# A hybrid decoder step on one core: the last expert block goes to a fifth plane of rows, four planes are summed by matrix products, and gate products move to the front of compression

## Chip, cores, metric

One Trainium2 chip, one of its cores. The metric is device time in microseconds (us) of one execution. GB/s and MB are decimal.

## What is computed

One layer of a decoder for 512 prompt tokens and 32 sample tokens (544 rows of 1024 values): projections, three gated branches (causal pooling, sparse attention, attention into a memory), an output product, and a mixture of experts. Two pieces of the reference matter here. The first makes the keys and values of the compressed branch from blocks of tokens, for 8 cached sequences and the prompt:

```python
sub = kv[:, :n_sub * CMP_STRIDE].reshape(b, n_sub, CMP_STRIDE, 2, NSA_KV_HEADS, HEAD_DIM)
for r in range(r_sub):
    part = jnp.einsum("bnjcgd,cjde->bncge", sub + pe_r, cmp_w[:, sl])[:, r:r + n_cmp]
```

The second is the end of the experts. Each row goes to 4 of 32 experts, and its four results are added, with gates, to the row itself:

```python
y = jnp.zeros((a, d), h.dtype).at[order].set(out_rows[dest]).reshape(n, TOP_K, d)
return jnp.einsum("nk,nkd->nd", gates, y)
x = x + moe(rmsnorm(x, p["norm2_g"]), p)
```

## The kernel before

The program is a row of phases with a barrier of all engines between them. Each engine has its own list of instructions, written out by hand; engines wait for each other by semaphores, and each engine carries out its list in order, its DMA issues among it. SBUF is one array (`arena`) whose regions are reused by hand; the trace names it `arena` throughout.

**Compression** (L1096 to L1341). For each of 8 sequences s, TensorE forms `products(s, 0)` and `products(s, 1)` (L1298) from cache pages that SP, ScalarE and GpSimd load, `blocks(s)` (L1311) and `keys(s)` (L1319, a transpose of `kn`). ScalarE's `after` (L1167 to L1170) and VectorE's `after` (L1240 to L1247) make `kn`, for which `keys` waits. ScalarE also issues page loads and loads of constants between its instructions (L457, L1200 to L1208). Into this phase five `gate_product`s (L1327) are put as filling: each is 16 products of 272 columns into two banks, which VectorE copies out (L1254) and ScalarE writes to memory (`scr_gate`, L1211). The order on TensorE for s from 1 to 5 is: products(s, 0), blocks(s-1), products(s, 1), keys(s-1), gate_product(s-1). TensorE starts with a wait for `s_bh`, VectorE's first instruction of the phase (L1232), and for weights (`s_cw`). The loads of the next phase (`in_cache_slc` on SP and GpSimd) wait until all five gate results are in memory (`f_s`).

**Gates and output product** (L2351 to L2638). 24 units of gate and branch products on TensorE (L2618, L2625), a sigmoid of ScalarE for each (L2417), VectorE multiplies and adds; SP loads the weights.

**Experts** (L2799 to L3062). Rows are packed into blocks of 96 slots, each block with one expert; with these inputs 32 blocks are used of 54 that the loops allow for. For each used block SP loads 12.6 MB of weights in three pieces into three ring slots (L2817), TensorE forms gate and up products (L2987) and down products (L3013) in three groups g of 32 slots, and ScalarE scales the result (L2906). GpSimd gathers the rows of the next block (L2853) and scatters this block's result (L2874) into `y_of`, which has one plane of rows for each of a row's 4 choices; `slot_row` holds where each slot goes. After the last used block each engine still steps through the unused turns of its loop.

At the end SP waits until all scatters of all blocks have landed (L2823), then loads the four planes of each tile of 128 rows (tile 4 has 32) and stores the finished tiles. VectorE adds the four planes to `x` one after another (L2969), the last tile in two halves of 512 columns (L2977). The list of VectorE:

```python
for n in ORDER[:-1]:
    for k in range(TOPK):
        if k % 2 == 0:
            dve.wait_ge((y_lo, y_hi)[k // 2][n], 16)
        ins = dve.tensor_tensor(x_end(n)[0:r], x_end(n)[0:r], four(n)[0:r, k], ALU.add)
```

Here `ORDER` is tile 4, then 0 to 3, and `four(n)` holds 4 planes of 1024 values on each of 128 partitions.

Of the kernel before, what the change touches and what calls it, by code (L numbers as in the profile page):

```python
# [22 lines left out]
D = 1024  # L23
# [4 lines left out]
NT = 5  # L28
# [189 lines left out]
def build_program(nc, i, o, stop_after=99):  # L218

    ctx = ExitStack()  # L220
    with ctx:
# [881 lines left out]
        with nc.Block() as block:  # L1103
# [50 lines left out]
            def _(act):  # L1154
# [33 lines left out]
                for s in range(NS):  # L1188
# [41 lines left out]
            def _(dve):  # L1230
# [17 lines left out]

                for s in range(NS - 1):
                    after(s)  # L1250
                    if s < FILL:
                        for h in range(2):
                            dve.wait_ge(f_p, 2 * s + h + 1)
                            dve.tensor_copy(fill_out[:, s, HALF * h:HALF * h + HALF], bank(h)[:, 0:HALF]).then_inc(f_e, 1)  # L1254
# [8 lines left out]
            def _(pe):  # L1263
                pe.wait_ge(s_bh, 1)
                pe.wait_ge(s_cw, 48)

# [1008 lines left out]
        b_down = take(D)  # L2275
        assert cursor[0] <= w_gb_at, cursor[0]
        scr_h = scratch("scr_h", [NTOK, D])
        y_of = scratch("y_of", [TOPK, 1024, D])
        hT_at = oT_at - 120 - KD * NTOK
        ring_at = [hT_at, tail_base + KD * D, tail_base]  # L2280
        end_at = [hT_at, hT_at + 4096, w_gb_at, tail_base + KD * D, tail_base + KD * D + 4096]
# [69 lines left out]
        with nc.Block() as block:  # L2351
# [55 lines left out]
            def _(act):  # L2407
                for u in range(24):
# [8 lines left out]
                    act.activation(two(sig[:, s]), gate, ACT.Sigmoid).then_inc(g_sg, 1)  # L2417
                for n in range(NT):
# [15 lines left out]
            def _(dve):  # L2434
                link = linked(dve, s_d5, [0])
                for u in range(24):
# [120 lines left out]
                dve.tensor_copy(n_used[:, 0:1], ends[:, NE - 1:NE])  # L2557

# [186 lines left out]
        cur_gate = take(4)  # L2745
        assert cursor[0] <= routing_base
# [20 lines left out]
        y_hi = [sem(f"y_hi{n}") for n in range(NT)]  # L2767
        y_half = [sem(f"y_half{h}") for h in range(2)]
        y_add = sem("y_add")
# [4 lines left out]
        ORDER = [NT - 1] + list(range(NT - 1))  # L2774
        GU_K = RING_W // 2048
# [3 lines left out]
        four = lambda n: arena[:, end_at[n]:end_at[n] + 4096].rearrange("p (k n) -> p k n", k=TOPK)  # L2779
        x_end = lambda n: x[:, n]  # L2780
        out_p = o["y_prompt"][0]
# [4 lines left out]
        def used(eng):  # L2786

            return eng.value_load(n_used[0:1, 0:1], min_val=1, max_val=NBLK)  # L2788
# [10 lines left out]
        with nc.Block() as block:  # L2799
            @block.sync  # L2800
            def _(sp):
                blocks = used(sp)
                sp.wait_ge(e_sent, 1)
# [18 lines left out]
                for g in range(G):  # L2822
                    sp.wait_ge(e_out[g], blocks * 16)  # L2823
                for n in ORDER[:-1]:
                    r = ROWS[n]
                    sp.dma_start(four(n)[0:r, 0:2], y_of[0:2, 128 * n:128 * n + r].rearrange("k t n -> t k n")  # L2826
                                 ).then_inc(y_lo[n], 16)
                    sp.dma_start(four(n)[0:r, 2:4], y_of[2:4, 128 * n:128 * n + r].rearrange("k t n -> t k n")  # L2828
                                 ).then_inc(y_hi[n], 16)
                last = ORDER[-1]  # L2830
                for h in range(2):
                    sp.dma_start(four(last)[:, :, 512 * h:512 * h + 512],
                                 y_of[:, 128 * last:128 * last + 128, 512 * h:512 * h + 512].rearrange("k t n -> t k n")
                                 ).then_inc(y_half[h], 16)
                for m, n in enumerate(ORDER[:-1]):
                    r = ROWS[n]
                    sp.wait_ge(y_done, m + 1)
                    sp.dma_start(out_p[128 * n:128 * n + 128] if r == 128 else out_s, x_end(n)[0:r]).then_inc(p_out, 16)
                for h in range(2):
                    sp.wait_ge(y_done, NT + h)  # L2840
                    sp.dma_start(out_p[128 * last:128 * last + 128, 512 * h:512 * h + 512], x_end(last)[:, 512 * h:512 * h + 512]
                                 ).then_inc(p_out, 16)
                sp.wait_ge(p_out, 16 * NT + 16)

            @block.gpsimd
            def _(pool):
# [13 lines left out]
                blocks = used(pool)  # L2860
                with pool.Fori(0, NBLK // 9) as nine:  # L2861
                    with pool.If(9 * nine < blocks):
                        with pool.Fori(0, 9) as one:
                            b = 9 * nine + one
                            with pool.If(b < blocks):
# [5 lines left out]
                                for g in range(G):  # L2871
# [3 lines left out]
                                                            y_rows[:, g], None, bounds_check=4 * 1024 * TOPK - 1, oob_is_err=False  # L2875
# [40 lines left out]
            def _(dve):  # L2916
# [13 lines left out]
                blocks = used(dve)  # L2930
                with dve.Fori(0, NBLK // 9) as nine:
# [31 lines left out]
                link = linked(dve, y_add, [0])  # L2963
                for n in ORDER[:-1]:
                    r = ROWS[n]
                    for k in range(TOPK):
                        if k % 2 == 0:
                            dve.wait_ge((y_lo, y_hi)[k // 2][n], 16)
# [107 lines left out]
```

## Time and profile before

| | us |
|---|---|
| median of 3 runs | 1854.88 (1852.64 to 1856.59) |
| the profiled execution, its own time | 1856.81 |
| its span, first to last instruction | 1854.8 |
| compression, first to last product | 175.5 to 300 |
| units of gates | 499 to 706 |
| experts, first to last product of TensorE | 815.6 to 1817.9 |
| behind the last product | 1817.9 to 1854.8 |

The profile is of one execution. Times in rows count from the span's start. PE is TensorE's products, PEld its weight loads, DVE VectorE, ACT ScalarE, POOL GpSimd, SP the engine that only issues DMAs; a q behind a name is the engine's issuing part. A float32 product appears as two rows of the trace.

### The profile page before, as it was taken

What the parts mean: (1) busy time and instruction counts of PE and PEld (TensorE: products, weight loads), DVE (VectorE), ACT (ScalarE), POOL (GpSimd) and SP (SyncE); (2) the same over time, 40 slices, a digit from 0 to 9 for tenths busy, and PEclk for the clock granted to TensorE, in tenths of its full rate; (3) what the DMA queues carried; (4) which work ended last, traced back from release to release, by engine and by line L of the source; (5) the groups of instructions that cost most, each with busy time, mean ns of one, the idle gap of its engine ahead of it and who ended that gap; (6) DMA issues with size and microseconds to landing.
All of it is one profiled execution on the core that took longest, in us unless ns stands there. A gap on an engine that the chain in (4) does not pass through costs nothing.

```text
span 1854.8 us, 40016 instructions
## 1 busy us (share of the span) xinstructions
PE 1714.4 (92%) x16080; PEld 953.3 (51%) x16080; DVE 550.5 (30%) x1391; ACT 338.1 (18%) x740; POOL 449.9 (24%) x520
## 2 busy tenths in 40 slices
PE   7998997679799999879999999999999999999992
PEld 3446785244478884534465754444444444444441
DVE  1333113446401113453232313231323232323235
ACT  3232112146400001101111111111111111111110
POOL 1122326647400006011212212221212222222220
PEclk9997997779999999879999999999999999999996
DMA  9534757850251103339999999999999999999986
GB/s 342 198 104 150 252 162 221 278 210 2 84 165 57 52 25 119 139 151 404 425 422 425 416 421 411 428 423 421 422 421 408 427 423 420 423 420 406 430 338 248
DMA packets 86641, 541.98 MB, mean 292 GB/s; under 512 B 19888, under 2 KB 44048, under 8 KB 73617
## 3 DMA queue, kind: packets, MB, share of 16 engines
q1 hardware_dynamic: 64809, 498.50, 66.8%
q0 software_dynamic: 14544, 32.03, 5.1%
q10 hardware_dynamic: 7232, 10.73, 1.8%
q8 instruction: 32, 0.52, 0.1%
q14 instruction: 24, 0.20, 0.0%
HBM read 523.39 MB, written 29.78 MB: 298 GB/s over the span
## 4 chain that ended last, share of the span: by engine, by line
PE 54%; DMA 1%; DVE 0%; issue 0%; SPq 0%; POOLq 0%; POOL 0%; ACT 0%
PE psum L2987 36%; PE psum L3013 18%; DMA arena<-y_of 1%; PE psum L2997 0%; DVE arena L2977 0%; SPq L2826 0%; SPq L2828 0%; DMA y_of<-arena 0%; DMA arena<-scr_h,arena 0%; DVE arena L2920 0%; POOL arena L2857 0%; POOLq L2788 0%; ACT arena L2906 0%; POOLq L2861 0%; POOLq L2857 0%
## 5 line engine op out<-in xcount | busy, mean ns | idle before, releaser
L2987 PE MATMUL psum<-arena 128*32 128x512 f32 x6144 | 668.2, 592 | 2.7 <-issue 2.7
L2987 PEld LDWEIGHTS psum<-arena 128*32 128x32 f32 x6144 | 234.4, 108 | 417.0 <-issue 413.3
L3013 PE MATMUL psum<-arena 128*32 128x256 f32 x6144 | 344.9, 378 | 0.0
L3013 PEld LDWEIGHTS psum<-arena 128*32 128x32 f32 x6144 | 236.0, 109 | 110.0 <-issue 9.6
L2942 DVE TENSOR_TENSOR arena<-psum,arena 128x512 f32<-128x512 f32 x96 | 66.5, 692 | 582.4 <-PE psum L2987 582.4
L2874 POOL DMA_INDIRECT y_of<-arena x96 | 97.0, 1011 | 476.2 <-ACT arena L2906 476.2
L2902 ACT ACTIVATE arena<-arena 128x256 f32<-128x256 f32 x96 | 40.1, 418 | 610.1 <-DVE arena L2944 610.1
L2618 PE MATMUL psum<-arena 128*128 128x272 f32 x608 | 144.3, 395 | 1.6 <-PEq L235 1.6
L2618 PEld LDWEIGHTS psum<-arena 128*128 128x128 f32 x608 | 116.1, 191 | 28.5 <-issue 3.3
L2853 POOL DMA_INDIRECT arena<-scr_h,arena x96 | 98.8, 1030 | 48.9 <-POOL arena L2849 28.2
L878 PE MATMUL psum<-arena 128*128 128x512 f32 (+1 forms) x256 | 97.4, 541 | 12.7 <-DMA arena<-in_w_tok 10.1
L2906 ACT ACTIVATE arena<-psum,arena 128x256 f32<-128x256 f32 x96 | 45.7, 476 | 245.7 <-PE psum L3013 245.7
L878 PEld LDWEIGHTS psum<-arena 128*128 128x128 f32 x256 | 46.1, 200 | 62.7 <-issue 60.6
L1984 POOL TENSOR_SCALAR arena<-arena 128x512 f32<-128x512 f32 (+3 forms) x64 | 68.5, 1085 | 20.0 <-DVE arena L2111 20.0
L462 POOL DMA_INDIRECT arena<-in_cache_slc,arena x60 | 59.2, 987 | 49.9 <-DMA scr_gate<-arena 26.2
L2444 DVE TENSOR_TENSOR arena<-psum,arena 128x544 f32<-128x544 f32 x24 | 17.4, 725 | 181.3 <-ACT arena L2417 174.6
L2849 POOL COPY arena<-arena 128x3 uint32 x32 | 6.1, 189 | 268.2 <-DMA y_of<-arena 238.1
L2920 DVE STREAM_TRANSPOSE arena<-arena 128x768 f32<-128x768 f32 x33 | 32.2, 977 | 120.5 <-DMA arena<-scr_h,arena 120.5
L2625 PE MATMUL psum<-arena 128*128 128x272 f32 x256 | 63.2, 398 | 3.6 <-DMA arena<-in_w_up 3.6
L462 POOL DMA_INDIRECT arena<-in_cache_cmp,arena x48 | 46.6, 970 | 76.1 <-PE psum L1298 33.8
L440 POOL CAST arena<-arena 32x8 bf16<-32x8 f32 (+1 forms) x6 | 6.2, 1033 | 240.7 <-DMA arena<-in_b_gu 219.8
L1298 PE MATMUL psum<-arena 128*128 128x256 f32 x256 | 61.2, 393 | 3.1 <-DVE arena L1232 3.1
(369 smaller groups left out, 1520.5 us busy)
## 6 DMA issues: line engine op xcount, KB each, us to landing
arena<-in_w_gu SPq DMA_DIRECT2D x64, 4096.0 KB, 15.1
arena<-in_w_down SPq DMA_DIRECT2D x32, 4096.0 KB, 14.5
arena<-in_w_gb SPq DMA_DIRECT2D x24, 512.0 KB, 4.5
arena<-y_of SPq DMA_DIRECT2D x8, 1024.0 KB, 15.3
arena<-in_cache_cmp SPq DMA_DIRECT2D x62, 128.0 KB, 3.1
arena<-in_cache_slc SPq DMA_DIRECT2D x60, 128.0 KB, 6.5
arena<-in_x_all SPq DMA_DIRECT2D x8, 512.0 KB, 11.3
arena<-in_w_tok SPq DMA_DIRECT2D x2, 2048.0 KB, 14.0
```

The lines of the kernel that those rows point to most:

```text
L462: pool.indirect_dma_start(dst, None, i[table], bass.IndirectOffsetOnAxis(page_row[:, at:at + 1], 0)).then_inc(sem, 16)
L878: mm = pe.matmul(bank(2 + c)[0:r, 0:b - a], dstT(n)[:, k], w_tok[:, k, a:b], start=(k == 0), stop=(k == KD - 1))
L1298: mm = pe.matmul(sum_bank(s, c)[:, 0:2 * n].rearrange("p (g b m) -> p g b m", g=2, b=PAGES), w_cmp[:, c, j], turned, start=(j == 0), stop= ...
L1984: ins = pool.tensor_scalar(rows, rows, c[:, g:g + 1], None, ALU.mult)
L2618: pe.matmul(bank(4 * s + h)[:, 0:HALF], w_gb[:, u % 6, k], hT[:, k, t], start=(k == 0), stop=(k == KD - 1))
L2625: mm = pe.matmul(bank(4 * s + 2 + h)[:, 0:HALF], w_up[:, k, 128 * c:128 * c + 128], oT_of(k)[:, t], start=(k == k0), stop=(k == k1 - 1))
L2853: pool.indirect_dma_start(xg[:, g], None, h_quarters, bass.IndirectOffsetOnAxis(row_from[:, g:g + 1], 0), bounds_check=4 * NTOK - 1, oob_i ...
L2874: pool.indirect_dma_start(y_quarters, bass.IndirectOffsetOnAxis(row_to[:, g:g + 1], 0), y_rows[:, g], None, bounds_check=4 * 1024 * TOPK - ...
L2906: act.activation(y_rows[:, g], dn_half(g), ACT.Copy, scale=cur_gate[:, g:g + 1]).then_inc(e_yc, 1)
L2942: dve.tensor_tensor(gu_c[:, g], gu_bank(g), bias_sb, ALU.add).then_inc(e_ba, 1)
L2987: mm = pe.matmul(gu_bank(g)[32 * j:32 * j + 32].rearrange("p (h n) -> p h n", h=2), xgT[:, g, 32 * k:32 * k + 32], gu_w(slot)[:, part, :, ...
L3013: mm = pe.matmul(dn_half(g)[32 * j:32 * j + 32], actT[:, g, 32 * k:32 * k + 32], dn_w(slot)[:, part, 256 * j:256 * j + 256], start=(k == 0 ...
```

## The change

Compression: `gate_product(0)` stands first on TensorE, ahead of the two waits; `gate_product(s)` for s from 1 to 4 stands between products(s, 1) and keys(s-1). VectorE's copies and ScalarE's loads of window keys (`load_window`) move with them, one turn earlier.

```diff
-                    if s == FILL + 1:
+                    if s == FILL:
+                        act.wait_ge(f_e, 2 * FILL)
                         act.wait_ge(s_spill, 16)
                         for n in range(4):
                             load_window(act, 0, n)
...
+                gate_out(0)
                 for s in range(NS - 1):
                     after(s)
...
+                    if s + 1 < FILL:
+                        gate_out(s + 1)
...
-                pe.wait_ge(s_bh, 1)
-                pe.wait_ge(s_cw, 48)
...
+                gate_product(0)
+                pe.wait_ge(s_bh, 1)
+                pe.wait_ge(s_cw, 48)
                 for s in range(NS):
                     products(s, 0)
                     if s:
                         blocks(s - 1)
                     products(s, 1)
+                    if 1 <= s < FILL:
+                        gate_product(s)
                     if s:
                         keys(s - 1)
-                    if 1 <= s <= FILL:
-                        gate_product(s - 1)
```

Gates phase: `y_of` gets a fifth plane, and all five planes are filled with zeros: VectorE clears 256 columns once, ScalarE issues 25 stores of them (one after each sigmoid, two after the first), 11.1 MB in all.

```diff
+                    if u == 0:
+                        act.wait_ge(z_z, 1)
+                    for m in range(u, NT * (TOPK + 1), 24):
+                        k, n = divmod(m, NT)
+                        act.dma_start(y_of[k, 128 * n:128 * n + ROWS[n]].rearrange("t (j n) -> t j n", j=4),
+                                      zeros[0:ROWS[n]].unsqueeze(1).to_broadcast([ROWS[n], 4, 256])).then_inc(z_w, 16)
```

Experts: VectorE rewrites the entries of `slot_row` of the last used block so that its rows go to the fifth plane, at their row number (L2957 of the new file). SP waits for the scatters of all blocks but the last (`rest`), then loads four planes of each tile in a new layout: one load for each plane k and tile, to the 32 partitions 32k to 32k+31, four rows on each. TensorE sums the planes with a matrix `stack` of four identities of 32 side by side, 8 products of 512 columns for a tile of 128 rows (2 for tile 4), VectorE adds the result from PSUM, and then the rows of the fifth plane, which SP loads once the last block's scatters have landed.

```diff
                 for g in range(G):
+                    sp.wait_ge(e_out[g], rest * 16)
+                for n in (0, 1, 4, 2, 3):
+                    if n == 2:
+                        sp.wait_ge(e_use, USES * blocks + USES)
+                    for k in range(TOPK):
+                        sp.dma_start(four(n)[32 * k:32 * k + 32],
+                                     y_of[k, 128 * n:128 * n + ROWS[n]].rearrange("(c t) n -> t c n", t=32)).then_inc(y_lo[n], 16)
+                for g in range(G):
                     sp.wait_ge(e_out[g], blocks * 16)
...
+                for n in ORDER:
+                    sp.dma_start(last_rows(n)[0:ROWS[n]], y_of[TOPK, 128 * n:128 * n + ROWS[n]]).then_inc(y_l[n], 16)
+                for m, n in enumerate(ORDER):
                     sp.wait_ge(y_done, m + 1)
+                    sp.dma_start(out_p[128 * n:128 * n + 128] if n < NT - 1 else out_s, x_end(n)[0:ROWS[n]]).then_inc(p_out, 16)
...
+                for m, n in enumerate(ORDER):
                     r = ROWS[n]
+                    for h in range(2):
+                        half = slice(512 * h, 512 * h + 512)
+                        dve.wait_ge(y_mm, 2 * m + h + 1)
+                        dve.tensor_tensor(x_end(n)[0:r, half], x_end(n)[0:r, half], bank(SUM_BANKS[m][h])[0:r], ALU.add
+                                          ).then_inc(y_ev, 1)
+                for m, n in enumerate(ORDER):
+                    r = ROWS[n]
+                    dve.wait_ge(y_ev, 2 * m + 2)
+                    dve.wait_ge(y_l[n], 16)
+                    dve.tensor_tensor(x_end(n)[0:r], x_end(n)[0:r], last_rows(n)[0:r], ALU.add).then_inc(y_done, 1)
...
+                for m, n in enumerate(ORDER):
+                    pe.wait_ge(y_lo[n], 16 * TOPK)
...
+                    for h in range(2):
+                        for c in range(CHUNKS[n]):
+                            mm = pe.matmul(bank(SUM_BANKS[m][h])[32 * c:32 * c + 32], stack, four(n)[:, c, 512 * h:512 * h + 512],
+                                           start=True, stop=True, tile_position=(0, 32 * c))
+                        mm.then_inc(y_mm, 1)
```

The order of TensorE at the front of compression, before (L1298 products, L1311 blocks, L1319 keys, L1327 gate product):

```order
L1262 UNCONDITIONAL_BRANCH
L1298 MATMUL psum<-arena 128x256 x24
L1311 MATMUL psum<-arena 127x64 x4
L1298 MATMUL psum<-arena 128x256 x8
L1319 MATMUL psum<-arena 128x127
L1327 MATMUL psum<-arena 128x272 x16
L1298 MATMUL psum<-arena 128x256 x8
L1311 MATMUL psum<-arena 127x64 x4
```

And in the change (L1300 products, L1313 blocks, L1321 keys, L1329 gate product):

```order
L1267 UNCONDITIONAL_BRANCH
L1329 MATMUL psum<-arena 128x272 x16
L1300 MATMUL psum<-arena 128x256 x24
L1313 MATMUL psum<-arena 127x64 x4
L1300 MATMUL psum<-arena 128x256 x8
L1329 MATMUL psum<-arena 128x272 x16
L1321 MATMUL psum<-arena 128x127
L1300 MATMUL psum<-arena 128x256 x8
```

A gate product now stands ahead of everything, and the next one ahead of the first keys.

The end of SP's list before, behind the loop over blocks (loads of planes, then stores):

```order
L2826 DMA arena<-y_of 32x2x1024
L2828 DMA arena<-y_of 32x2x1024
L2826 DMA arena<-y_of 128x2x1024
L2828 DMA arena<-y_of 128x2x1024
...
L2832 DMA arena<-y_of 128x4x512 x2
L2838 DMA out_y_sample<-arena 32x1024
L2838 DMA out_y_prompt<-arena 128x1024 x3
L2841 DMA out_y_prompt<-arena 128x512 x2
```

And in the change:

```order
L2855 DMA arena<-y_of 32x4x1024 x8
L2855 DMA arena<-y_of 32x1024 x4
L2853 REGISTER_ALU
L2855 DMA arena<-y_of 32x4x1024 x8
L2858 REGISTER_ALU
L2860 DMA arena<-y_of 32x1024
L2860 DMA arena<-y_of 128x1024 x4
L2863 DMA out_y_sample<-arena 32x1024
L2863 DMA out_y_prompt<-arena 128x1024 x4
```

Twenty loads, each to 32 partitions, have taken the place of ten, most of them to 128 partitions; five loads of the fifth plane stand behind them.

## Rows read from the trace of the kernel before

**Rows 1.** The page's second part: GB/s of the DMAs in 40 slices.

```profile
GB/s 342 198 104 150 252 162 221 278 210 2 84 165 57 52 25 119 139 151 404 425 422 425 416 421 411 428 423 421 422 421 408 427 423 420 423 420 406 430 338 248
```

**Rows 2.** The chain that ended last, in time: start us, us, what.

```profile
1810.97 6.94 PE psum L3013 x128
...
1819.26 2.35 DMA y_of<-arena
...
1827.00 19.13 DMA arena<-y_of
...
1851.12 0.69 DVE arena L2977
```

**Rows 3.** Windows: stretch, us, busy PE PEld DVE ACT POOL, clock, DMA share, GB/s.

```profile
1799.00:1818.00 19.00, 18.88 (x276) 9.63 (x268) 8.62 (x19) 2.76 (x7) 4.93 (x7) 1.00 0.05 17
...
1828.00:1838.00 10.00, 0.00 (x0) 0.00 (x0) 9.12 (x8) 0.00 (x0) 0.00 (x0) 0.50 1.01 405
```

**Rows 4.** Waits of SP's queue: total us, times, longest.

```profile
SPq L2823 <- DMA y_of<-arena: 22.4, 1, 22.4
```

**Rows 5.** Compression, TensorE and others in order: start us, us, what [idle before <- releaser].

```profile
175.52 13.51 PE L1298 MATMUL psum<-arena 128*128 128x256 f32 x48 [3.12 <-DVE arena L1232]
...
197.62 0.33 PE L1319 MATMUL psum<-arena 127*128 127x127 f32 x1 [4.22 <-DVE arena L1247]
197.78 9.19 PE L1327 MATMUL psum<-arena 128*128 128x272 f32 x32
206.81 3.64 PE L1298 MATMUL psum<-arena 128*128 128x256 f32 x16
...
214.76 7.50 PE L1327 MATMUL psum<-arena 128*128 128x272 f32 x32
```

**Rows 6.** The same of SP, ScalarE, VectorE and GpSimd.

```profile
186.28 15.20 SPq L457 DMA_DIRECT2D arena<-in_cache_cmp  x14
...
194.72 0.96 ACT L1185 ACTIVATE arena<-psum,arena 64x254 f32<-64x254 f32 x2 [8.17 <-issue]
...
197.27 0.29 DVE L1247 TENSOR_TENSOR arena<-arena 127x128 f32<-127x128 f32 x1
...
279.05 0.94 POOL L462 DMA_INDIRECT arena<-in_cache_slc,arena  x1 [26.16 <-DMA scr_gate<-arena]
```

**Rows 7.** Windows as in rows 3, in compression behind TensorE's wait.

```profile
198.00:202.00 4.00, 4.00 (x12) 2.99 (x11) 0.00 (x0) 0.28 (x1) 2.28 (x3) 0.57 0.85 260
```

**Rows 8.** Windows, the phase of gates.

```profile
515.00:706.00 191.00, 189.38 (x825) 155.57 (x823) 28.70 (x40) 15.06 (x24) 0.00 (x0) 1.00 0.23 71
```

**Rows 9.** ScalarE in the phase of gates: group, busy us, mean ns, idle before.

```profile
L2417 ACT ACTIVATE arena<-arena 128x544 f32<-128x544 f32 x5 | 3.3, 657 | 5.1 <-DVE arena L2444 5.1
```

**Rows 10.** Windows of half a us while loads to 32 partitions run.

```profile
530.50:531.00 0.50, 0.50 (x4) 0.42 (x3) 0.00 (x0) 0.00 (x0) 0.00 (x0) 1.00 1.05 205
...
708.50:709.00 0.50, 0.50 (x2) 0.34 (x1) 0.00 (x0) 0.00 (x0) 0.00 (x0) 0.50 0.87 164
...
1824.50:1825.00 0.50, 0.00 (x0) 0.00 (x0) 0.00 (x0) 0.00 (x0) 0.00 (x0) 0.50 0.73 139
```

**Rows 11.** Groups of products and of VectorE: busy us, mean ns, idle before.

```profile
L2987 PE MATMUL psum<-arena 128*32 128x512 f32 x6144 | 668.2, 592 | 2.7 <-issue 2.7
L2942 DVE TENSOR_TENSOR arena<-psum,arena 128x512 f32<-128x512 f32 x96 | 66.5, 692 | 582.4 <-PE psum L2987 582.4
```

**Rows 12.** VectorE at the end, in order of time.

```profile
1843.52 2.48 DVE L2969 TENSOR_TENSOR arena<-arena 128x1024 f32<-128x1024 f32 x2 [0.16 <-DMA arena<-y_of]
```

**Rows 13.** The DMA list: out<-in queue op xcount, KB each, us to landing.

```profile
arena<-in_b_down SPq DMA_DIRECT2D x4, 128.0 KB, 4.4
y_of<-arena POOLq DMA_INDIRECT x96, 8.1
```

**Rows 14.** One line of SP's: its two last loads of planes.

```profile
L2832 SPq DMA_DIRECT2D arena<-y_of x2: 3189/4004/4819, 1827.0 to 1830.2; - x2
...
DMA to landing us min/median/max: 18.6/18.9/19.1
```

More of the change, by code:

```diff
@@ L1247, in after, with gate_out @@
                     dve.tensor_tensor(kn[0:n], kn[0:n], gain_kc[0:n], ALU.mult).then_inc(s_kn, 1)
+                def gate_out(j):
+                    for h in range(2):
+                        dve.wait_ge(f_p, 2 * j + h + 1)
+                        dve.tensor_copy(fill_out[:, j, HALF * h:HALF * h + HALF], bank(h)[:, 0:HALF]).then_inc(f_e, 1)
+                gate_out(0)
                 for s in range(NS - 1):
                     after(s)
[L1251 to L1254, printed above, removed]
+                    if s + 1 < FILL:
+                        gate_out(s + 1)
                 for q in (1, 3):
@@ L2435, in _ @@
                 link = linked(dve, s_d5, [0])
+                dve.memset(zeros, 0.0).then_inc(z_z, 1)
                 for u in range(24):
@@ L2557, in _ @@
                 dve.tensor_copy(n_used[:, 0:1], ends[:, NE - 1:NE])
+                dve.tensor_scalar(n_used[:, 1:2], ends[:, NE - 1:NE], -1.0, None, ALU.add)
                 dve.wait_ge(r_rank, 1)
@@ L2745, in build_program @@
         cur_gate = take(4)
+        stack = take(32)
         assert cursor[0] <= routing_base
@@ L2766, in build_program @@
         y_lo = [sem(f"y_lo{n}") for n in range(NT)]
-        y_hi = [sem(f"y_hi{n}") for n in range(NT)]
-        y_half = [sem(f"y_half{h}") for h in range(2)]
-        y_add = sem("y_add")
+        y_l = [sem(f"y_l{n}") for n in range(NT)]
+        y_mm, y_ev, y_st, y_lr = sem("y_mm"), sem("y_ev"), sem("y_st"), sem("y_lr")
         y_done = sem("y_done")
@@ L2802, in _ @@
                 blocks = used(sp)
+                rest = rest_of(sp)
                 sp.wait_ge(e_sent, 1)
@@ L2860, in _ @@
                 blocks = used(pool)
+                pool.wait_ge(z_w, 16 * NT * (TOPK + 1))
+                pool.wait_ge(y_lr, 1)
                 with pool.Fori(0, NBLK // 9) as nine:
@@ L2930, in _ @@
                 blocks = used(dve)
+                to_last = slot_row[:, bass.ds(rest_of(dve), 1)]
+                dve.tensor_scalar(to_last, to_last, 4095, LAST_PLANE, ALU.bitwise_and, ALU.bitwise_or).then_inc(y_lr, 1)
+                dve.tensor_tensor(stack, ident[:, 0:32], ident[:, 32:64], ALU.add).then_inc(y_st, 1)
+                for k in (2, 3):
+                    dve.wait_ge(y_st, k - 1)
+                    dve.tensor_tensor(stack, stack, ident[:, 32 * k:32 * k + 32], ALU.add).then_inc(y_st, 1)
                 with dve.Fori(0, NBLK // 9) as nine:
@@ L3060, in _ @@
                         pe.nop()
+                pe.wait_ge(y_st, 3)
+                pe.wait_ge(e_ba, blocks * G)
+                for m, n in enumerate(ORDER):
+                    pe.wait_ge(y_lo[n], 16 * TOPK)
+                    if m == 1:
+                        pe.wait_ge(e_yc, blocks * G + G)
+                        pe.wait_ge(e_bc, blocks + 1)
+                    if m == NT - 1:
+                        pe.wait_ge(y_ev, 2)
+                    for h in range(2):
+                        for c in range(CHUNKS[n]):
+                            mm = pe.matmul(bank(SUM_BANKS[m][h])[32 * c:32 * c + 32], stack, four(n)[:, c, 512 * h:512 * h + 512],
+                                           start=True, stop=True, tile_position=(0, 32 * c))
+                        mm.then_inc(y_mm, 1)
 def kernel(**inputs):
```

58 lines of the change are left out of this document (17 added, 41 removed).

## The prediction

> **What bounds the kernel now.** I read the slices of the page first. From the 19th slice to the 38th the DMA engines move 404 to 430 GB/s [rows 1]: that is the experts, where the weights stream all the time, and the change leaves that loop alone. It touches three places, so I looked at what each waits for there.
>
> The end: the chain of waits. The last product ends at 1817.9 (1810.97 + 6.94). ScalarE scales it, the last scatter goes out at 1819.26 and lands 2.35 us later, SP then issues the plane loads, the longest piece of the chain is 19.13 us of such a load, and VectorE's last add ends at 1851.8 [rows 2]. The reader is to see that 36.9 us pass behind the last product, and that most is the loading of 8.9 MB. Meanwhile the DMA engines did nothing while TensorE computed the last block: share 0.05 from 1799 to 1818 [rows 3]. SP stood ready all that time: it waited 22.4 us for the scatters, until about 1821.6, so since 1799.2 [rows 4].
>
> The front of compression: TensorE waits 3.12 us for VectorE's first instruction, then later 4.22 us for `kn` ahead of the first keys, and the gate product behind that takes 9.19 us where the next takes 7.50 [rows 5]. `kn` is late because ScalarE was issuing loads for 8.17 us [rows 6]. The longer gate product is the clock: 0.57 granted from 198 to 202, after the idle stretch [rows 7].
>
> The phase of gates: TensorE is busy 189.4 of 191 us there, and the DMA share is 0.23 at 71 GB/s [rows 8].
>
> **Compression, worked out.** VectorE's instruction that releases TensorE starts as soon as the barrier opens and takes 0.23 us, so the 3.12 us are barrier, not L1232: moving the gate product ahead gains 0.3 us at most. The first three sets of products took 13.51 us where a warm set takes 3.5 (3.64 with its tail) [rows 5]: 3.1 us go to the half clock at the phase's start, and the gate product pays them instead. The 4.22 us go: gate product 0 takes 7.5 + 3.1 = 10.6 us from 175.2, three warm sets 10.4, blocks and the fourth set 4.3, so gate product 1 starts at 200.5 and ends at 208.0. ScalarE's chain moves later with the first products. `kn` depends on ScalarE, whose loads run until about 201.6, and on the 2.8 us between ScalarE's restart at 194.72 and `kn` at 197.56 [rows 6]: 204.4, 3.6 us ahead of need. The clock loss of 1.7 us (9.19 - 7.50) [rows 5] goes with the wait. Sum 4.2 + 1.7 = 5.9 gained, 0.1 to 0.3 either way at the front: I take **5.8**. Five gate products are the same work.
>
> What is late next? Loads of pages wait for products that end up to 7 us later at the start. Those of sequences 3 and 4, issued from 186.3 for 15.2 us [rows 6], now go out from 193, and sequence 3 is needed at 223.6, so nothing waits; from sequence 5 on everything runs 5.8 earlier. The loads of the next phase wait for the last gate result in memory [rows 6]. ScalarE stores it at the same turn of its list as before, so this moves by the same 5.8, not by a whole turn. The window loads are moved ahead of it; that costs nothing, since their new wait (`f_e`) is over when the turn comes, and takes 2 MB out of a busy stretch: a gain between 0 and 2 us, taken as 0.
>
> **Zeros.** 25 stores, 11.1 MB. Over the 191 us of that phase this is 58 GB/s beside 71, against more than 400 that the engines can do: hidden behind TensorE, which waits for weights asked for some 50 us ahead. Issuing costs ScalarE some 0.45 us each. The tightest place is the last five sigmoids, where ScalarE still idles 5.1 us in all [rows 9], more than 5 x 0.45 = 2.3. Cost 0; if the cover were gone, at most 11.1 MB / 0.4 = 28 us, which nothing in rows 8 suggests. The register loads, `stack` and the rewritten `slot_row` lie behind the barrier of the experts while SP's and TensorE's first block runs for 30 us: 0. GpSimd waits for `y_lr` ahead of its gather for block 1, needed 30 us later: 0.
>
> **The end, worked out.** SP now asks only for all blocks but the last. That block's last scatter is a period of 31.2 earlier than 1819.26, at 1788.1, and lands 8.1 later [rows 13], 1796.2. So the first load goes out when SP leaves its loop, 1799.3. The four planes are 4 x 544 x 4096 B = 8.91 MB. The new layout decides the rate: each load writes 32 partitions. What does the trace show of such loads? The four loads of `in_b_down` go to partitions 0, 32, 64 and 96 in turn, the very pattern of the change [rows 13], and in the half microsecond where their packets of 4 KB fill the engines these are busy 1.05 and move only 205 GB/s [rows 10]; the three of `in_b_gu`, also 32 partitions each, give 164 at share 0.87 [rows 10]. Loads to 128 partitions give 405 at share 1.01 [rows 3]. So full engines, half the bytes. The bounds are thus 139 (tile 4's loads at the end of before, share 0.73 [rows 10]) and 405; I take 215, a little over the 205 of the full share, because where the loads change from the first two quarters to the last two, engines ahead and behind need not share.
>
> The Trainium skill says why it may be so: "SBUF — State Buffer", section "Door 1: The DMA port swizzle", has 32 partitions reach only 8 of 16 ports. By its 436 GB/s the rate would be an estimated 218, which speaks against the new layout. The slice at 205 agrees with it.
>
> Landing of tile 3's planes: 1799.3 + 2.4 (an empty queue's delay, as of the scatter in rows 2) + 8.91/0.215 = 41.5 + 0.4 for the last scatters = **1843.6**. Before, the last piece landed at 1830.2 + 18.6 = 1848.8 [rows 14], 5.2 us later: all the head start of 22 us but this is eaten by the rate. Behind the landing: 8 products, each two rows of 0.109 us (668.2/6144 [rows 11]), are 1.7 us at full clock, and 3.5 at half; TensorE has idled some 8 us between tiles, and when idle it stands at 0.50 [rows 3], so 3.5. Then one eviction of 0.69 [rows 11], and five adds of the fifth plane of 1.24 (2.48/2 [rows 12]) with gaps, 6.3, because VectorE's list has all of these behind the last eviction. The fifth plane itself (2.2 MB, 5.5 us) lands by 1851, ahead of the last add, which starts at 1853. Then the store: before, 1854.8 - 1851.8 = 3.0 for 256 KB, now 512 KB, 3.6. With 0.2 for the waits: 0.2 + 3.5 + 0.7 + 6.3 + 3.6 = 14.3, where before it was 6.0. End: 1843.6 + 14.3 = 1857.9, that is **3.1 later** than 1854.8.
>
> **Sum.** -5.8 + 3.1 = -2.7. The profiled execution took 1856.8 (its span 1854.8 and 2.0 around it), so 1854.1; the median of the runs is 1.9 lower: **1852.2**.
>
> **Rivals.** *Full rate:* the loads run at 405. 22 us put the planes there at 1824.1; then the fifth plane decides. Its scatter lands between 1822 and 1827.4 (2.35 to 8.1 us), its loads take 2.4 + 5.5, last add and store 4.9: end near 1838.5, 16.3 earlier, 22.1 in all, 1832.8. For it: only few microseconds of the trace show such loads, and they are small. Against: three places agree on half. *Engines drift apart:* neighbours end up in different quarters, 300 GB/s or so, 29.7 us, landing 1831.8, end 1846.1: -14.5 in all, 1840.4. For it: nothing couples the engines. Against: nothing drives them apart either. The Trainium skill, "DMA: Bandwidth & Descriptors", section "Rules for kernel authors", speaks against it: transfers to disjoint halves of the partitions serialize. By that rule it would be the 215 above. *Slower:* the rate stays at what 708.5 shows, 164 GB/s [rows 10]. Then 54.3 us, landing 1856.4, end 1870.7, +15.9 - 5.8 = +10.1: 1865.0. From 186 GB/s down it is measurably slower, and 202 is the point of no gain. For it: rows at 139 and 164; against: these have a share below 1. *Compression gives nothing,* because a page load comes late: +3.1 alone, 1858.
>
> **Chances.** A measurement here tells 0.2%, 3.7 us, from no change. Forecast (186 to 230 GB/s) 0.56, full rate 0.15, drift 0.14, slower rival 0.12, no gain in compression 0.03. Faster needs over 220 GB/s: 0.15 + 0.14 + 0.15 of the forecast's 0.56 = 0.44. Same: the other 0.41 and 0.02. Slower: 0.13. The forecast's own range is 1848 to 1858; to leave out no more than 2 in 10 the range takes in drift and full rate: 1832 to 1859.
>
> **What would show it.** In compression no idle ahead of the first keys, first gate product about 10.6 us, all later starts 5.8 earlier. Loads of planes issued from about 1793.5, DMA share 1 with 205 to 220 GB/s until the planes are in; the sums of tile 3 at half clock; five adds in a row as VectorE's last work; TensorE no longer idle at the end. GB/s near 400 there, or planes landed before 1826, would prove me wrong, and so would a wait of TensorE in the phase of gates.

## The result, and the profile after

The change was 3.4 us slower by the medians, 3.5 by the ratio: median 1858.41 us of 20 runs (1854.99 to 1862.68) beside 1855.02 of 20 runs of the kernel before (1851.39 to 1859.28), ratio 1.0019 with a 95% interval of 1.0013 to 1.0025. Forecast was 2.7 us faster. The time lies inside the stated range (1832 to 1859), but the direction was wrong. The profiled execution of the change has a span of 1857.9. Ratios here and below leave out two executions that took far longer than all others, one of c_all (3050.04 us) and one of the kernel before (2632.61).

**The end.** SP's list, start us, us, what:

```profile
1798.81 18.84 SPq L2855 DMA_DIRECT2D arena<-y_of  x20
1826.98 2.20 SPq L2860 DMA_DIRECT2D arena<-y_of  x5
1849.87 0.35 SPq L2863 DMA_DIRECT2D out_y_sample<-arena  x1
1851.01 3.74 SPq L2863 DMA_DIRECT2D out_y_prompt<-arena  x4
```

Windows, with columns as in [rows 3]:

```profile
1799.00:1818.00 19.00, 18.35 (x272) 8.43 (x260) 8.45 (x19) 3.17 (x7) 4.43 (x6) 1.00 0.96 201
1828.00:1838.00 10.00, 5.86 (x42) 1.23 (x34) 4.55 (x7) 0.00 (x0) 0.00 (x0) 0.94 1.03 209
1844.00:1848.00 4.00, 3.64 (x16) 0.59 (x16) 0.69 (x1) 0.00 (x0) 0.00 (x0) 0.50 1.02 397
```

TensorE and VectorE at the end:

```profile
1810.26 7.09 PE L3036 MATMUL psum<-arena 128*32 128x256 f32 x128
1824.11 7.83 PE L3095 MATMUL psum<-arena 128*32 128x512 f32 x36 [6.76 <-DMA arena<-y_of]
1834.36 1.93 PE L3095 MATMUL psum<-arena 128*32 128x512 f32 x16 [2.42 <-DMA arena<-y_of]
1844.32 3.64 PE L3095 MATMUL psum<-arena 128*32 128x512 f32 x16 [8.04 <-DMA arena<-y_of]
```

```profile
1848.03 0.69 DVE L2997 TENSOR_TENSOR arena<-arena,psum 128x512 f32<-128x512 f32 x1 [1.02 <-PE psum L3095]
1848.64 5.75 DVE L3003 TENSOR_TENSOR arena<-arena 32x1024 f32<-32x1024 f32 x5
```

The 19 us in which the DMA engines stood idle before [rows 3] are now full (share 0.96), but at 201 GB/s. From 1828 to 1838 the loads to 32 partitions move 209 at share 1.03, where [rows 3] has 405; as soon as the fifth plane comes, whose loads go to 128 partitions, it is 397. The last planes are there at 1844.3, TensorE sums them at half clock (granted 0.50), and VectorE has five adds left. Behind the last product (1810.26 + 7.09 = 1817.35) pass 40.5 us, before 36.9: 3.6 more.

The last block's scatter took 8.15 us to land beside the plane loads, the far end of the 2.35 to 8.1 that the prediction allowed:

```profile
1818.75 8.15 DMA y_of<-arena
```

It held nothing up. The five loads of the fifth plane went out from 1826.98 and landed from 1844.8 to 1849.7, each ahead of its add.

**The front of compression.** TensorE:

```profile
175.03 10.30 PE L1329 MATMUL psum<-arena 128*128 128x272 f32 x32 [2.83 <-PEq L235]
185.16 10.60 PE L1300 MATMUL psum<-arena 128*128 128x256 f32 x48
...
199.97 7.49 PE L1329 MATMUL psum<-arena 128*128 128x272 f32 x32
207.30 0.27 PE L1321 MATMUL psum<-arena 127*128 127x127 f32 x1
```

No idle time stands ahead of the first keys (4.22 us in [rows 5]), and the second gate product takes 7.49 us at full clock. The last keys of the phase start at 294.05; before, at 300.00:

```profile
300.00 0.31 PE L1319 MATMUL psum<-arena 31*128 31x31 f32 x1 [1.81 <-DVE arena L1247]
```

So 5.9 us were gained inside the phase. The next phase's first product, before and then after:

```profile
305.45 0.76 PE L1714 MATMUL psum<-arena 128*128 128x127 f32 x2 [5.14 <-DVE arena L1533]
```

```profile
302.76 0.77 PE L1719 MATMUL psum<-arena 128*128 128x127 f32 x2 [8.40 <-DVE arena L1538]
```

Only 2.7 are left, and TensorE's wait is 3.3 us longer. In front of that product stand the page loads of SP and GpSimd, which wait for the last gate result in memory: 26.4 us pass from GpSimd's first such load to the product before (279.05 to 305.45), 26.5 after. ScalarE's queue and GpSimd's first load, after:

```profile
262.37 2.62 ACTq L1045 DMA_DIRECT2D arena<-in_win_kt  x4
...
269.42 0.33 ACTq L1211 DMA_DIRECT2D scr_gate<-arena  x1
```

```profile
276.26 0.95 POOL L462 DMA_INDIRECT arena<-in_cache_slc,arena  x1 [22.77 <-DMA scr_gate<-arena]
```

Before, the store went out at 276.14, and GpSimd followed at 279.05 [rows 6], 2.9 later. Now the store goes out at 269.42, 6.7 earlier, but GpSimd can start only 6.8 later: four window loads of 512 KB each were put ahead of the store in the same queue.

```profile
276.14 0.33 ACTq L1211 DMA_DIRECT2D scr_gate<-arena  x1
```

The last store's time from issue to landing (view of L1211, window 262:280), before and then after:

```profile
DMA to landing us min/median/max: 2.1/2.1/2.1
```

```profile
DMA to landing us min/median/max: 6.1/6.1/6.1
```

So the store itself landed 4.0 us later after its issue, which is the difference between 2.9 and 6.8.

**The zeros.** TensorE's phase of gates is as busy as in [rows 8], with nearly twice the traffic:

```profile
515.00:706.00 191.00, 189.37 (x827) 155.62 (x826) 29.12 (x42) 15.16 (x24) 0.00 (x0) 1.00 0.41 130
```

### The profile page after: what moved, and what is told of

Same layout as the page of the kernel before. It is cut to its first block, busy times and chain, and to the rows that moved or that the text cites. A ratio compares the mean times of both kernels' runs of the same rounds, so it can differ in the third digit from the quotient of the medians.

```text
span 1857.9 us, 40208 instructions
## 1 busy us (share of the span) xinstructions
PE 1730.7 (93%) x16148; PEld 958.7 (52%) x16148; DVE 539.5 (29%) x1388; ACT 338.1 (18%) x740; POOL 450.8 (24%) x520
## 4 chain that ended last, share of the span: by engine, by line
PE 54%; DMA 2%; issue 0%; DVE 0%; SPq 0%; DVEq 0%; POOLq 0%; POOL 0%; ACT 0%
PE psum L3010 36%; PE psum L3036 18%; DMA arena<-y_of 1%; DMA y_of<-arena 0%; PE psum L3020 0%; DVE arena L3003 0%; DMA arena<-scr_h,arena 0%; SPq L2860 0%; DVEq L2825 0%; DVE arena L2943 0%; POOL arena L2878 0%; POOLq L2810 0%; ACT arena L2929 0%; POOLq L2878 0%; POOLq L2901 0%
## 5 line engine op out<-in xcount | busy, mean ns | idle before, releaser
L1300 PE MATMUL psum<-arena 128*128 128x256 f32 x256 | 58.3, 379 | 0.0
```

The costliest lines, as they stand in the source:

```text
L1300: mm = pe.matmul(sum_bank(s, c)[:, 0:2 * n].rearrange("p (g b m) -> p g b m", g=2, b=PAGES), w_cmp[:, c, j], turned, start=(j == 0), stop= ...
```

## The experiments

Twelve kernels ran, planned in three groups, each beside runs of the kernel before on the same chip. When the first group was planned, I compared the last product of the two profiles (1817.88 before, 1817.35 after) and thought that of the 2.7 us at the start of the next phase only 0.5 survived. Start times in the texts and the table are each from one profiled execution.

### Parts alone: end_only, c_all, c_late

end_only is the change without its part in compression. c_all is the kernel before with only that part. c_late is c_all with one edit taken back:

```diff
-                    if s == FILL:
-                        act.wait_ge(f_e, 2 * FILL)
+                    if s == FILL + 1:
                         act.wait_ge(s_spill, 16)
                         for n in range(4):
                             load_window(act, 0, n)
```

> The change without its part in compression: zeros, fifth plane and sum by products stay. Theory: the end alone costs 3.1 to 3.6 us, the zeros nothing, so the last product ends at 1817.9 as before and the time is 3 to 4 us over that of the kernel before (+0.17 to +0.21%). Rival (the zeros or the rewriting of slot_row slow something): more than 4.5 us over before, and the last product ends later than 1818.5. Second rival (compression gains nothing at all in the change): the same time as the change.

> The kernel before with the part in compression alone (gate products moved, window loads moved a turn earlier). Theory (the gain inside compression is handed back behind it): the last keys end 5.9 us earlier, the first product of the next phase only 2.7, the last product of the experts 0.3 to 0.8 earlier: time 0 to 0.8 us under before (ratio 0.9996 to 1.0000). Rival (the gain survives, and the rest of the change eats it): 2.7 to 5.8 us under before, ratio 0.9969 to 0.9985.

> As c_all, but the window loads stay at their old turn, behind the store of the last gate result in ScalarE's queue. Theory (the four loads of 0.5 MB ahead of that store held it back by 4 us): the store lands 2.9 us after its issue instead of 6.8, the loads of the next phase start 5 to 6 us earlier than before (near 273 to 274), and its first product starts near 299.7, 5.8 earlier than before instead of 2.7. In the total this leaves between 0.5 and 5.8 us, depending on what later phases absorb. Rival (the store is late for another reason): GpSimd's first gather at 276.3 as in c_all, first product at 302.8.

| kernel | median us | ratio to before, 95% | GpSimd's first page load | first product of next phase |
|---|---|---|---|---|
| before | 1854.01 | | 279.05 | 305.45 |
| end_only | 1858.40 | 1.0023 (1.0014 to 1.0032) | 277.08 | 303.47 |
| c_all | 1852.42 | 0.9982 (0.9972 to 0.9992) | 276.29 | 302.67 |
| c_late | 1848.67 | 0.9968 (0.9957 to 0.9979) | 270.87 | 297.26 |

end_only came near the theory: 4.4 us over before by the medians, 4.3 by the ratio, where 3 to 4 were expected. From the first product of the next phase to the last product of the experts it took 1511.8 us (303.47 to 1815.22), before 1512.4 (305.45 to 1817.88), so the zeros held nothing up there.

c_all missed. It is 1.6 us faster by the medians and 3.3 by the ratio (1.5 to 5.2), whose interval leaves out my 0 to 0.8; by the ratio it is in the rival's range. My theory that later phases hand the gain back rested on one execution of each kernel. How wrong that is shows end_only, whose compression is the old code: its next phase starts 2 us earlier than before's in the profile. The stretch from the first product of that phase (305.45 in the row of before above) to the first product that waits for GpSimd's L1984 shows the same. Before and end_only, the same code:

```profile
407.40 1.97 PE L2173 MATMUL psum<-arena 128*128 128x128 f32 x8 [5.90 <-POOL arena L1984]
```

```profile
403.75 1.97 PE L2173 MATMUL psum<-arena 128*128 128x128 f32 x8 [6.46 <-POOL arena L1984]
```

It took 101.9 us in one and 100.3 in the other, and between 99.7 and 103.9 over all kernels here. A difference of 2 us there, between single profiles, says nothing.

c_late bore the theory of the window loads out: the store leaves at 267.99, and 2.9 us later GpSimd starts, 26.4 us ahead of the next phase's first product.

```profile
267.99 0.33 ACTq L1211 DMA_DIRECT2D scr_gate<-arena  x1
```

```profile
270.87 0.94 POOL L462 DMA_INDIRECT arena<-in_cache_slc,arena  x1 [18.82 <-DMA scr_gate<-arena]
```

```profile
297.26 0.77 PE L1718 MATMUL psum<-arena 128*128 128x127 f32 x2 [5.17 <-DVE arena L1537]
```

That is 8.2 us ahead of before, where 5.8 were expected, and the time fell by 5.3 (medians) to 5.9 us (ratio). The 2.4 more are no more than the spread between executions: TensorE's whole list stood 1.4 us earlier here than in the profile of the change, and in end_only, the second profile with the old compression, the store left at 274.20 and not 276.14.

### The cause inside the change: change_late

This is the change itself with the edit of c_late, and nothing else.

> The change with the window loads alone back at their old turn of ScalarE's list. It tests the step of the prediction that took their move as free. Theory: GpSimd's first page load at 271 instead of 276.3, first product of the next phase near 297 to 298 instead of 302.8, and 2 to 4 us off the change: 1854.5 to 1856.5, ratio to before 0.9998 to 1.001. Rival (it was the transfers of the phase behind, not the store, that took the gain): 1858 again.

Measured: 1852.44 us, ratio 0.9992 (0.9983 to 1.0001), where the change had 1.0019 (1.0013 to 1.0025). GpSimd's first load starts at 271.69, the first product at 298.07. So moving the window loads back takes 5 us (ratios, 3 to 7 with both intervals) to 6 (medians) off the change. The theory had the place and the two start times right; of its size, 2 to 4 us, the measurement leaves only the upper part. The end is what it was: the last product ends at 1809.6, the span at 1850.5, 40.9 us behind it.

```profile
1802.50 7.11 PE L3035 MATMUL psum<-arena 128*32 128x256 f32 x128
```

### Which partitions: wide, near, far, near_rows

wide loads 32 rows of all four planes at once, so that partition 4t+k holds row t of plane k (`stack` and the wait counts are made to match in this and the next kernels):

```diff
-                    for k in range(TOPK):
-                        sp.dma_start(four(n)[32 * k:32 * k + 32],
-                                     y_of[k, 128 * n:128 * n + ROWS[n]].rearrange("(c t) n -> t c n", t=32)).then_inc(y_lo[n], 16)
+                    for c in range(CHUNKS[n]):
+                        sp.dma_start(four(n)[:, c], y_of[0:TOPK, 128 * n + 32 * c:128 * n + 32 * c + 32].rearrange("k t n -> t k n")
+                                     ).then_inc(y_lo[n], 16)
```

> The change, with the plane loads laid out over all 128 partitions: partition 4t+k holds row t of plane k, so that each load writes 128 partitions, and the matrix of ones that sums them is made to match. Bytes, products, waits and additions are the same. Theory (the 200 to 209 GB/s of the changed kernel come from loads that each write 32 partitions): about 400 GB/s, planes landed near 1824 instead of 1843.6; then the fifth plane decides, whose scatter landed at 1826.9, and the span ends 14 to 20 us earlier than that of the change, 1838 to 1844. Rival (the rate comes from reading y_of row by row, or from packets of 4 KB): 200 GB/s still, the same end within 2 us, 1856 to 1860.

Measured: 1841.71 us, ratio 0.9926 (0.9913 to 0.9940).

```profile
1807.00:1811.00 4.00, 4.00 (x80) 2.44 (x76) 1.34 (x3) 0.96 (x2) 1.04 (x1) 1.00 1.02 407
1811.00:1815.00 4.00, 4.00 (x80) 2.32 (x76) 0.00 (x0) 0.48 (x1) 1.00 (x1) 1.00 1.02 410
```

```profile
1819.55 10.45 PE L3096 MATMUL psum<-arena 128*32 128x512 f32 x68 [4.15 <-issue]
```

The same bytes in the same packets of 4 KB come at 407 to 410 GB/s. TensorE's sums wait for no DMA any more, and run as one piece. Behind the last product (1815.4) pass 24.6 us where the change has 40.5: 16 us are the price of the layout.

The next three ask whether the number of partitions counts or which ones. near has two loads for each 32 rows, to partitions 0 to 63 and 64 to 127. far has two loads as large, to every second partition of all 128.

```diff
+                        for k in (0, 2):
+                            sp.dma_start(four(n)[32 * k:32 * k + 64, c], y_of[k:k + 2, 128 * n + 32 * c:128 * n + 32 * c + 32]).then_inc(y_lo[n], 16)
```

```diff
+                        for k in (0, 1):
+                            sp.dma_start(four(n)[k::2, c], y_of[k:TOPK:2, 128 * n + 32 * c:128 * n + 32 * c + 32].rearrange("k t n -> t k n")
+                                         ).then_inc(y_lo[n], 16)
```

> The change with two planes to a load, each load to 64 neighbouring partitions (0 to 63, then 64 to 127), in the old layout of planes. Twice as many partitions per load as in the change, half as many as in wide. Theory A (what counts is which partitions a load writes together: 0 to 63 share the same paths as 0 to 31): 200 to 215 GB/s still, planes landed near 1843, end as in the change, 1856 to 1860. Theory B (the rate goes by the number of partitions or of rows in flight): 300 to 400 GB/s, planes landed before 1832, end 1838 to 1848.

> The change in the layout of wide, two loads to a chunk, each to every second partition of all 128: 64 partitions per load as in near, the same 256 KB in packets of 4 KB, but spread from 0 to 127. Theory A (which partitions): about 400 GB/s, planes landed near 1824, end as wide, 1838 to 1844. Theory B (how many partitions): the same rate as near, whatever that is. Near and far apart show A, alike show B.

far (two runs) came as theory A had it: 1841.90 us, 0.9933 (0.9915 to 0.9951). near (two runs) did what no theory had: 1988.74 us, 1.0725 (1.0706 to 1.0745). Far, then near:

```profile
1815.00:1819.00 4.00, 2.33 (x44) 1.28 (x36) 0.00 (x0) 0.47 (x1) 1.29 (x2) 1.00 1.02 402
```

```profile
1830.00:1840.00 10.00, 0.00 (x0) 0.00 (x0) 0.00 (x0) 0.00 (x0) 0.00 (x0) 0.50 0.13 52
```

A share of 0.13 is 2 of the 16 DMA engines. The outermost count of near's source is 2 (planes), far's is 32 (rows). So near does not answer its question, and near_rows repeats it with rows outermost:

```diff
+                        for h in (0, 1):
+                            sp.dma_start(four(n)[64 * h:64 * h + 64, c],
+                                         y_of[2 * h:2 * h + 2, 128 * n + 32 * c:128 * n + 32 * c + 32].rearrange("k t n -> t k n")
+                                         ).then_inc(y_lo[n], 16)
```

> The fair partner of far: the same two loads of 256 KB to a chunk, rows outermost in the source as there, but one load goes to partitions 0 to 63 (planes 0 and 1 side by side) and the other to 64 to 127. Near ran at a DMA share of 0.13, 2 of 16 engines, because its outermost count in the source was 2; here that is 32. Theory A (what counts is which partitions are written together): all engines busy, share 1.0, 200 to 215 GB/s, end as in the change, 1856 to 1860. Theory B (how many partitions): 340 to 410 GB/s as far, end 1840 to 1844.

Measured: 1851.92 us, ratio 0.9988 (0.9978 to 0.9998).

```profile
1803.00:1807.00 4.00, 4.00 (x72) 2.45 (x68) 3.06 (x7) 0.42 (x1) 0.00 (x0) 1.00 1.06 246
...
1827.00:1831.00 4.00, 1.93 (x16) 0.42 (x16) 1.38 (x2) 0.00 (x0) 0.00 (x0) 1.00 1.04 245
```

All engines are busy and move 245 GB/s: above theory A's 200 to 215, far below B's 340 to 410. With as many partitions to a load, spread ones give 402 and neighbouring ones 245, so it is above all which partitions are written together. The 40 GB/s over theory A came where the halves alternate from load to load; in the change they alternate after every second load. That neighbouring loads overlap a little is my reading; no run tells it from another cause.

### The two mends together: best_late, best_early, wide_late, wide_early

best_late was to be the change with one load of 128 partitions for each 32 rows, planes outermost, and the window loads back. best_early has ScalarE's stores of gate results a turn earlier as well.

```diff
-                    if 2 <= s < FILL + 2:
-                        act.wait_ge(f_e, 2 * (s - 1))
-                        act.dma_start(scr_gate[s - 2], fill_out[:, s - 2]).then_inc(f_s, 16)
+                    if 1 <= s < FILL + 1:
+                        act.wait_ge(f_e, 2 * s)
+                        act.dma_start(scr_gate[s - 1], fill_out[:, s - 1]).then_inc(f_s, 16)
```

> The change with both flaws mended: each load of planes goes to all 128 partitions (the four planes of 32 rows in one load, so that the layout and the matrix of identities stay), and the window loads are back at their old turn. Theory: the gains of wide (about 1841.7) and of the mended compression (another 2.6, c_late against c_all) add: 1838 to 1840.5, ratio to before 0.991 to 0.9927. Rival (a gain of compression is taken up by the transfers of the phase behind it when the zeros run too): as wide, 1841 to 1843.

> best_late with ScalarE's stores of gate results one turn earlier. The last gate result would be in memory some 6 to 8 us sooner, so the page loads of the next phase start near 263 to 265 instead of 271. Theory (these loads set the start of the next phase): its first product moves up from 297.3 by 3 to 7 us, and the time falls by as much, to 1832 to 1837. Rival (the keys, which end at 294, or the barrier behind them become the bound): first product not before 296.5, time as best_late within 1.5 us. Second rival (a wait of ScalarE for the VectorE copy delays its own chain and so the keys): slower than best_late.

Measured: 1902.29 (1.0266, 1.0252 to 1.0280) and 1902.18 us (1.0255, 1.0239 to 1.0271), more than 60 us over what was expected. Both sources have the four planes outermost, and the window of best_late shows what that costs:

```profile
1830.00:1840.00 10.00, 0.00 (x0) 0.00 (x0) 0.00 (x0) 0.00 (x0) 0.00 (x0) 0.50 0.26 103
```

Share 0.26 is 4 of 16 engines. Counts of 2, 4 and 32 gave shares of 0.13, 0.26 and 1, at about 26 GB/s for each engine. The Trainium skill, "DMA: Bandwidth & Descriptors", section "Why a DMA increments its semaphore by 16 and not by 1", states this: the number of engines is the largest up to 16 that divides the slowest dimension of both sides. The three shares agree with it.

So the two mends were put on wide instead.

> Wide (all 128 partitions, rows outermost) with the window loads at their old turn. Theory (gains add): 1841.7 less 2 to 4, so 1837.5 to 1840, ratio to before 0.991 to 0.9925. Rival: 1841 to 1843 as wide.

> Wide_late with ScalarE's stores of gate results one turn earlier. Theory (page loads of the next phase set its start): last gate result in memory near 263, first product of the next phase between 290 and 295, time 2 to 6 us under wide_late. Rival (the last keys at 294 and the barrier become the bound): first product not before 296, time within 1.5 us of wide_late. Second rival: ScalarE waits for the VectorE copy, its chain to the keys is late, slower than wide_late.

wide_late: 1836.08 us, ratio 0.9902 (0.9887 to 0.9917). The theory had 1837.5 to 1840. Against wide's 0.9926 that is 4.4 us, with 3.7 either way, so the gains add as far as these runs can tell. This is 18 us under the kernel before and 22 under the change.

wide_early: 1833.67 us, 0.9887 (0.9872 to 0.9902). In its profile the page loads start 4.3 us earlier than in wide_late (266.60 against 270.92), but the last keys and the first product come later:

```profile
295.30 0.31 PE L1320 MATMUL psum<-arena 31*128 31x31 f32 x1 [1.81 <-DVE arena L1247]
```

```profile
298.24 0.76 PE L1718 MATMUL psum<-arena 128*128 128x127 f32 x2 [2.64 <-DVE arena L1537]
```

In wide_late the keys stand at 292.56 and the product at 297.30. But this execution of wide_early entered the phase late already; its first product of compression and wide_late's:

```profile
178.14 9.26 PE L1328 MATMUL psum<-arena 128*128 128x272 f32 x32 [2.84 <-PEq L235]
```

```profile
174.68 9.26 PE L1328 MATMUL psum<-arena 128*128 128x272 f32 x32 [2.84 <-PEq L235]
```

Counted from there, the next phase starts after 120.1 us in wide_early and 122.6 in wide_late. best_early and best_late have the same two lists in compression, and give 120.1 and 122.6 as well. There the page loads start 7.3 us earlier (263.67 against 270.96) and the product 2.05 (295.30 against 297.35):

```profile
292.36 0.31 PE L1320 MATMUL psum<-arena 31*128 31x31 f32 x1 [1.81 <-DVE arena L1247]
...
295.30 0.76 PE L1718 MATMUL psum<-arena 128*128 128x127 f32 x2 [2.63 <-DVE arena L1537]
```

In the other twelve profiles, the kernel before included, the product follows GpSimd's first page load by 26.3 to 26.5 us; in these two it follows by 31.6, and the last keys by 2.94. So the bound moved from the page loads to TensorE's own list, as the rival had it, and of the earlier loads 2 to 2.5 us are left at the start of the phase. In the total the four runs of each don't tell wide_early from wide_late; whether the earlier store gains anything there stays open.

## Why the prediction was wrong

**The step that failed** is in the part on compression: "The window loads are moved ahead of it; that costs nothing, since their new wait (`f_e`) is over when the turn comes". I asked only whether ScalarE would wait, not what stands ahead of the store in its queue. The store of 272 KB landed 2.1 us after its issue before, 6.1 behind 2 MB of window loads, and 2.1 again with these behind it (c_late, change_late). With the wait for that store goes the start of the page loads, and 26.4 us behind it the next phase. Three pairs of kernels differ by this edit alone, and by the ratios it cost 5.0 us (change against change_late), 2.6 (c_all against c_late) and 4.4 (wide against wide_late), each within 2 to 4 us either way: all agree with the 4 us of the delay. No run put the window loads into another queue, so it is not shown whether their place in the queue counts or only their load on the DMA engines (share 1.03 to 1.05 from 266 to 272 in the change).

The step "ScalarE stores it at the same turn of its list as before, so this moves by the same 5.8" was sound. ScalarE did not wait for VectorE's copy at that turn, before or after. Before, the copy was made at 268.6 and the store went out right behind the start of an activation that waits for TensorE's products, at 276.14:

```profile
268.18 0.44 DVE L1254 COPY arena<-psum 128x272 f32<-128x272 f32 x1 [3.23 <-PE psum L1327]
```

```profile
276.02 0.47 ACT L1185 ACTIVATE arena<-psum,arena 64x254 f32<-64x254 f32 x1 [1.56 <-PE psum L1298]
```

In the change the same activation starts at 269.30 and the store at 269.42, so the store moves with TensorE's list: by 6.7 between these two profiles, and by 4.7 to 9.4 between the two profiles of the old list and the ten of the new one.

The mended account does not close. -2.7 and 4.0 for the delay and 0.5 for the end (3.6 instead of 3.1) make +1.8 us; measured was 3.5 (2.4 to 4.6). Taking back this one edit gives 1852.44, beside a forecast of 1852.2, but by the ratio that is 1.5 us under the kernel before and not 2.7; that the two times agree to 0.2 is luck.

**What held.** Inside compression: 10.30 us for the first gate product (10.6 said; 9.26 in c_late, where the clock rose earlier: 0.74 granted from 176 to 180, 0.50 in the change), no idle ahead of the keys, no page load late, and 5.9 at the last keys (5.8 said). That the last agrees to 0.1 is luck: the last keys stand at 298.82 and 300.00 in the two profiles of the old list, and between 290.4 and 294.1 in those of the new one with the window loads moved. The end: 209 GB/s (215 said), last planes at 1844.3 (1843.6), half clock in the last sums, five adds in a row, 3.6 us for the end (3.1). Two signs failed: the plane loads went out at 1798.81 and not 1793.5, since the last product came only 0.5 us earlier than before, and TensorE was idle at the end, 8.04 us ahead of its last sum, as the working itself had said and its list of signs had not. The head start of 22 us was eaten by the rate, as worked out; that the rate is the layout's doing was argued then, and wide, far and near_rows show it. The zeros: from the first product that waits for L1984 to the start of the product of L2700 before and L2718 after, the phases took 382.5 to 382.6 us in the three kernels without zeros, 383.5 in the change, and from 381.7 to 383.7 in the other kernels with zeros, so no cost of theirs above about 1 us is to be seen.

**The rivals.** Full rate was to end at 20.6 us behind the last product (1838.5 - 1817.9). wide, which has that rate, took 24.6: I had let the fifth plane decide, and left out that TensorE's sums start only at 1819.6, when it has stepped through its unused turns, and that VectorE's ten additions from PSUM and five of the fifth plane follow in one row. Compression gives nothing (1858) hit the time, but largely by luck: by itself compression did give 1.5 to 5.2 us (c_all), and what it lost it lost to a store behind other loads, not to a late page.

**What stays open.** c_all and end_only add up to 1 us over before (ratios 0.9982 and 1.0023), and the change measured 3.5 over. Each has an interval of 1 to 2 us either way, so these can be the same; I have no run that tells. In its profile the change lost 2.2 us to before between the first product of the next phase and the last product (1514.6 against 1512.4), and the same stretch took 1510.6 to 1514.6 over all kernels here; whether the change is to blame for any of it is not shown.

## What to carry to other kernels

Where an edit moves a DMA issue forward, ask more than whether its engine waits: list the transfers that it now stands ahead of, and find who waits for those. Spread a transfer's destination over all partitions (402 to 410 GB/s here, against 201 to 246), and keep all DMA engines at work by the outermost count of both its sides; the DMA share beside the GB/s in a window tells which of the two is wrong (full share and half the bytes, or a small share). And where a stage varies by 2 us between executions of the same code, no account of 2 us can be drawn from two profiles: run the part alone, many times.

## What the runs showed of the hardware that I had not expected

- The order of dimensions, with the same bytes and packets of 4 KB, changed the rate of loads to 128 partitions from 410 GB/s (rows outermost, 32: wide) to 103 (planes outermost, 4: best_late), and of loads to 64 neighbouring ones from 245 (near_rows) to 52 (planes outermost, 2: near).
- Loads to partitions 0 to 63 and 64 to 127 in turn gave 245 GB/s, about a fifth more than the 201 to 209 of the change. The Trainium skill, "SBUF — State Buffer", section "Can I just issue two DMAs to hit both halves?", has two such loads gain 6% over one. The gain here is larger, and still far from the 402 of spread partitions.
